# Moving a second context's statistics, some modulation products and the additions of the norms' squares in a fused two-block kernel on one core

## The chip, the core and the metric

The kernel runs on one core of a Trainium2 chip. A core has five engines that run their own instruction streams side by side and meet at semaphores: TensorE (PE in the profile; its weight loads are PEld), VectorE (DVE), ScalarE (ACT), GpSimd (POOL) and SyncE (SP, which here only issues transfers). The metric is the device time of one execution, in microseconds (us); lower is better.

## The reference

Two blocks are computed one after the other on 256 tokens of width 1024, all in float32. A second context `ctx_2` is normalised in the second block only.

```python
def rmsnorm(x, g):
    return x * lax.rsqrt(jnp.mean(x * x, axis=-1, keepdims=True) + EPS) * g

def modulate(h, shift, scale):
    return h * (1 + scale) + shift

# first block, layer 0: x += gate * (even mixer: conv branch and LRU branch, then w_out)
# first block, layer 1: x += gate * (odd mixer):
#     u, g = split(modulate(rmsnorm(x, ..)) @ od_w_in)            tiles "ou" and "og"
#     d    = multiscale_pool(u) - u
#     y    = einsum("bngi,gij->bngj", d, w_grp) * scale * silu(g)  tiles "grp"
#     out  = y @ od_w_out                                          tiles "oa" and "ob"
# x = rmsnorm(x, final_g)

# second block
# mod, mc = silu(c_2) @ w_mod_2 + b, silu(c_ctx_2) @ w_mod_2 + b
# hc = modulate(rmsnorm(ctx_2, g_mix), mc[0], mc[1])
# h  = modulate(rmsnorm(x, g_mix), mod[0], mod[1])
#     both times w_in_2                                           tiles "f", "i", "q", ...
# HGRN2 recurrence, gated unit with a layer norm of v, w_o, residual, rmsnorm
# SwiGLU: tiles "ua", "ub", then w_down; residual, rmsnorm(g_final)
```

## The kernel before, in words

Activations stand feature by feature: `x` is [128 partitions, 8 chunks, 256 tokens], so a chunk is a 128x256 float32 tile and a sum over the model width is a sum over partitions and over the 8 chunks (`KT` is 8). All weights come through one stream of 512 KB tiles, [128, 8, 128], in the fixed list `ORDER`. SP loads them into a ring of six buffers `raw`. For most tiles ACT rounds a copy `w_hi` (L868), DVE makes the rest `w_lo = raw - w_hi` (L1225), and PE makes three matmuls for each of the 8 chunks: high by high (L510), low by high (L511), high by low (L512), 24 for a tile. `thirds("oa", t, ...)` is that for tile t of the weights called "oa"; four banks `ps0` to `ps3` take turns as its results, and four more, `px`, take statistics and small products. The "grp" tiles are used as they come, from `raw` (L645). PE, ACT and DVE each go through their code in a fixed, hand-written order and wait on counting semaphores.

DVE makes `w_lo` a few tiles ahead: `lows(name, t)` makes all that are still missing up to that tile, and `ahead` calls it for the tile four further on, each time DVE is about to wait for a finished tile.

Between the parts of the model that multiply by weights there are norms. For a norm ACT squares the 8 chunks into a buffer (`sq1`, `sq2`, `sqc`, ...), counting `sq_ready`; PE sums them by 8 matmuls with a matrix of ones (`stats`, L474; a float32 matmul of 256 columns is listed as two records); DVE scales the sum (`rstd`, L1542), ACT takes the root (`sqrt_of`, L1056, behind a small activation on `warm`, L1052, that brings in its table), DVE inverts it (L1544), and `modulate` (DVE L1245 and L1250, ACT between them) makes the high and low halves of the next input. The norm of x behind the first block and the one that opens the second block are made together from `sq2` and `sqc` (L1652 to L1660).

The modulation vectors are products of a vector with `mod_w`, 80 tiles of 512 KB in 20 groups of four. POOL issues their loads in the order of `MOD_ORDER` into four buffers `modw` (L434), each when DVE has released that buffer, and DVE multiplies a tile by `c_row` and accumulates (`mod_tiles`, L1259; the second block's with two vectors, `second_mods`, L1580).

In program order, around the change: tiles "yb" with `add_to_x` (L1533) and the squares `sq1`; "ou" (16 tiles); "og" (16 tiles, DVE running `second_mods` beside them); "grp" (8 tiles, 128 matmuls); `stats` of `sqc`, here the squares of the second context `ctx2T`, which ACT makes behind its "grp" loop; "oa" 0 to 3, "ob" 0 to 3, "oa" 4 to 7, "ob" 4 to 7, with `add_to_x`, `sq2` and `sqc` (now squares of x) for each "ob" tile; the first "f" tile on the context; `stats` of `sq2` and of `sqc`; three more "f" tiles on the context and then those tiles on x; the rest of "f" on both. Much later come the sums of `v2` and `vsq` for the layer norm of v (L778, four matmuls each), `sq4` before "ua", and `sq5` at the end.

```python
def stats(bank, squares, ready, signal=sq_ready, tiles=KT, step=1):
    for k in range(tiles):
        pe.wait_ge(signal, ready + step * k + 1)
        last = pe.matmul(bank[:, 0:T], ones, squares(k), start=(k == 0), stop=(k == tiles - 1))
    last.then_inc(stat_done, 1)
```

## Time and profile before

| | before |
|---|---|
| median of 3 runs | 1001.12 us (1000.72 to 1001.75) |
| the profiled execution: time, span | 1004.44 us, 1002.7 us |
| mean granted TensorE clock | 0.957 of full |
| PE busy | 92% of the span |
| DVE busy | 71% |
| ACT busy | 50% |
| POOL busy | 11% |
| DMA, mean | 195 GB/s |

The profile is of one execution. "Busy" counts an engine's own instructions; PE at 92% may still wait at single places, and those are found in the timeline, where a row carries in brackets the idle time ahead of it and what ended it. PEclk is the TensorE clock that was granted, 1.00 for full speed.

### The profile page before, as it was taken

Reading aid. Unit: us, or ns where it says so; the run is one execution under the profiler, and the core shown is the slowest. Engines: PE = TensorE matmul, PEld = TensorE weight load, DVE = VectorE, ACT = ScalarE, POOL = GpSimd, SP = SyncE. Lnnn points to the kernel's source line nnn. Section 1 sums busy time; section 2 is a strip of 40 time slices with the busy share of each in tenths; the row PEclk is TensorE's granted clock in tenths of the full one; section 3 lists DMA queues with packets and bytes.
Section 4 is the critical chain, followed back from the end, with each engine's and each line's share of the span. In section 5 each row is a group of like instructions: output and inputs, shape, how many; then the busy total and the mean of one; then the engine's idle time right before and its main releaser. Section 6 shows DMA issues by size and latency. Waiting matters only on the chain.

```text
span 1002.7 us, 17148 instructions
## 1 busy us (share of the span) xinstructions
PE 920.5 (92%) x7040; PEld 855.5 (85%) x7040; DVE 709.1 (71%) x1061; ACT 501.2 (50%) x723; POOL 105.6 (11%) x212
## 2 busy tenths in 40 slices
PE   6799998798799999898899799998999899999996
PEld 3488676578798999887899799998999799999996
DVE  2986678936946599986755997666797695656543
ACT  4633889674734654224354348374543544444441
POOL 0003866500000000110100210000000000000000
PEclk9699999998799899998999899999999899999998
DMA  9734997942356368883861775453555376666661
GB/s 375 309 110 142 343 295 229 326 137 76 111 184 204 127 181 281 291 280 102 309 183 31 283 254 148 124 193 92 185 187 170 104 254 186 183 179 187 194 204 44
DMA packets 56014, 195.53 MB, mean 195 GB/s; under 512 B 7936, under 2 KB 9088, under 8 KB 54528
## 3 DMA queue, kind: packets, MB, share of 16 engines
q1 hardware_dynamic: 40320, 147.83, 46.1%
q0 software_dynamic: 15616, 46.61, 13.6%
q8 instruction: 56, 0.92, 0.4%
q14 instruction: 22, 0.18, 0.1%
HBM read 188.70 MB, written 1.05 MB: 189 GB/s over the span
## 4 chain that ended last, share of the span: by engine, by line
PE 63%; DVE 18%; DMA 7%; ACT 5%; issue 4%; POOL 2%; SPq 1%; DVEq 0%; ACTq 0%; POOLq 0%
PE ps L510 18%; PE ps L512 18%; PE ps L511 18%; DVE w_lo L1225 4%; DMA modw<-in_mod_w 3%; DVE modw L1259 2%; DMA m<-in_mod_w 2%; PE px L474 2%; POOL shifts L443 2%; DMA raw<-in_stream 2%; ACT w_hi L868 2%; DVE dump L1580 1%; PE ps L578 1%; PE px L567 1%; PE ps L645 1%
## 5 line engine op out<-in xcount | busy, mean ns | idle before, releaser
L1225 DVE TENSOR_TENSOR w_lo<-raw,w_hi 128x1024 fp32r<-128x1024 f32 x232 | 279.7, 1221 | 151.2 <-ACT w_hi L868 150.3
L510 PE MATMUL ps<-h_hi,w_hi 128*128 128x256 f32 (+1 forms) x928 | 281.2, 303 | 41.7 <-DVE w_lo L1225 26.3
L868 ACT ACTIVATE w_hi<-raw 128x1024 fp32r<-128x1024 f32 x232 | 243.3, 1055 | 129.6 <-DMA raw<-in_stream 129.4
L511 PE MATMUL ps<-h_lo,w_hi 128*128 128x256 f32 (+1 forms) x928 | 277.0, 298 | 0.0
L512 PE MATMUL ps<-h_hi,w_lo 128*128 128x256 f32 (+1 forms) x928 | 276.6, 298 | 0.0
L510 PEld LDWEIGHTS ps<-h_hi,w_hi 128*128 128x128 f32 x928 | 185.3, 200 | 52.9 <-DVE w_lo L1225 33.9
L511 PEld LDWEIGHTS ps<-h_lo,w_hi 128*128 128x128 f32 x928 | 185.4, 200 | 3.5 <-issue 0.7
L512 PEld LDWEIGHTS ps<-h_hi,w_lo 128*128 128x128 f32 x928 | 185.2, 200 | 2.7
L510 PE MATMUL ps<-h2o_hi,w_hi 128*128 128x256 f32 x352 | 103.2, 293 | 8.2 <-DVE w_lo L1225 8.2
L434 POOL DMA_DIRECT2D modw<-in_mod_w x80 | 42.8, 536 | 626.1 <-DVE modw L1259 357.8
L512 PE MATMUL ps<-h2o_hi,w_lo 128*128 128x256 f32 x352 | 100.9, 287 | 0.0
L511 PE MATMUL ps<-h2o_lo,w_hi 128*128 128x256 f32 x352 | 100.9, 287 | 0.0
L1259 DVE SCALAR_TENSOR_TENSOR modw<-modw,c_row 128x1024 f32<-128x1024 f32 x64 | 75.5, 1219 | 11.7 <-DMA modw<-in_mod_w 11.6
L510 PEld LDWEIGHTS ps<-h2o_hi,w_hi 128*128 128x128 f32 x352 | 68.9, 196 | 9.4 <-DVE w_lo L1225 8.6
L443 POOL DMA_DIRECT2D shifts<-upad x128 | 62.7, 498 | 73.9 <-DVE upad L1378 66.6
L511 PEld LDWEIGHTS ps<-h2o_lo,w_hi 128*128 128x128 f32 x352 | 68.9, 196 | 0.3 <-issue 0.2
L512 PEld LDWEIGHTS ps<-h2o_hi,w_lo 128*128 128x128 f32 x352 | 68.8, 196 | 0.0
L1043 ACT ACTIVATE sq<-x 128x256 f32<-128x256 f32 x32 | 13.4, 417 | 75.7 <-DVE x L1533 73.9
L510 PE MATMUL ps<-ff_hi,w_hi 128*128 128x256 f32 x176 | 49.8, 283 | 0.0
L511 PE MATMUL ps<-ff_lo,w_hi 128*128 128x256 f32 x176 | 49.8, 283 | 0.0
L512 PE MATMUL ps<-ff_hi,w_lo 128*128 128x256 f32 x176 | 49.8, 283 | 0.0
L510 PE MATMUL ps<-y_hi,w_hi 128*128 128x256 f32 x128 | 37.2, 291 | 3.5 <-DVE w_lo L1225 3.5
(308 smaller groups left out, 1717.9 us busy)
## 6 DMA issues: line engine op xcount, KB each, us to landing
raw<-in_stream SPq DMA_DIRECT2D x252, 512.0 KB, 3.9
modw<-in_mod_w POOLq DMA_DIRECT2D x80, 512.0 KB, 6.0
m<-in_mod_w SPq DMA_DIRECT2D x8, 1024.0 KB, 16.2
shifts<-upad POOLq DMA_DIRECT2D x128, 35.5 KB, 4.9
c_row<-in_c_rows SPq DMA_DIRECT2D x3, 512.0 KB, 7.7
ctxT<-in_ctxT SPq DMA_DIRECT2D x1, 1024.0 KB, 5.1
x<-in_xT SPq DMA_DIRECT2D x1, 1024.0 KB, 7.1
ctx2T<-in_ctx2T SPq DMA_DIRECT2D x1, 1024.0 KB, 7.5
```

Source lines behind the costliest of these rows:

```text
L434: pool.dma_start(modw[j][:], ins["mod_w"][t]).then_inc(modw_in[j], 16)
L443: pool.dma_start(shifts[t % 2][32 * d:32 * d + 32, g, :], upad[32 * g:32 * g + 32, t % 3, d:d + RW]).then_inc(shifts_in[t % 2], 16)
L474: last = pe.matmul(bank[:, 0:T], ones, squares(k), start=(k == 0), stop=(k == tiles - 1))
L510: pe.matmul(o, wh, hi, start=start, stop=False)
L511: pe.matmul(o, wh, lo, start=False, stop=False)
L512: return pe.matmul(o, wl, hi, start=False, stop=stop)
L567: mm = pe.matmul(px[b][:, :], w[:, 4 * e + b, :], xpad[:, head, :, SCONV_LEFT:SCONV_LEFT + T], start=True, stop=True)
L578: mm = pe.matmul(o[c, 0:T], w[:, n, c], shifts[t % 2][:, g, 4 * n:4 * n + T], start=(n == 0), stop=(n == QUADS - 1))
L868: act.activation(w_hi[split[0] % HI_RING][:], raw[n % RING][:], ACT.Copy).then_inc(w_hi_ready, 1)
L1043: act.activation(dst[:, t, :], x[:, t, :], ACT.Square).then_inc(sq_ready, 1)
L1225: v.tensor_tensor(w_lo[n % RING][:], raw[n % RING][:], w_hi[split[0] % HI_RING][:].bitcast(F32), ALU.subtract).then_inc(w_lo_ready, 1)
L1259: v.scalar_tensor_tensor(out=modw[s][:], in0=modw[s][:], scalar=1.0, in1=c_row[:, row, :], op0=ALU.mult, op1=ALU.mult, accum_out=mod[:, t: ...
```

## The change

It has three parts.

1. **Additions on GpSimd.** A new helper `add_up` makes POOL add chunks 1 to 6 of a buffer of squares into chunk 0, one 128x256 addition each, waiting for `sq_ready` of the chunk and for its own addition before. PE then sums two chunks by `two_chunks`: chunk 0 when `added` says that all six additions are made, and chunk 7. So it is for `sq1`, `sqx` (below), `sq2`, `sqc`, `sq4` and `sq5`; `v2` and `vsq` (four chunks) are added up entirely by POOL, three additions each, and PE takes one matmul for each. In all 36 + 6 = 42 additions. They stand in POOL's queue between the `modw` loads of groups 7 and 8 (`sq1`), 10 and 11 (`sqx`), 12 and 13 (`sq2` and `sqc`, taking turns), 16 and 17 (v), 18 and 19 (`sq4`) and behind the last loads (`sq5`).
2. **The context's statistics.** Its squares go to a buffer of their own, `sqx`, and ACT makes them before the tile "og" 10; PE sums them behind the last "og" tile, ahead of "grp"; ACT takes the root and DVE the inverse ahead of their "grp" loops. DVE's `modulate` of the context stands behind its "grp" loop as before, but behind two pieces of `lows` that now stand ahead of it.
3. **The modulation products.** `MOD_ORDER` becomes the plain order: groups 6 and 7 are loaded and multiplied at the "yb" tiles, no longer behind the context's `modulate`. Group 13 is multiplied one tile at a time in the first loop over `Kk`, no longer as one block of four ahead of it.

```diff
-MOD_ORDER = [0, 1, 2, 3, 4, 5, 8, 9, 10, 11, 6, 7] + list(range(12, MOD_TILES // MOD_SLOTS))
+MOD_ORDER = list(range(MOD_TILES // MOD_SLOTS))
...
+            def add_up(bufs, signal, ready, n, step=1):
+
+                before = [0] * len(bufs)
+                for k in range(1, n):
+                    for e, (dst, src) in enumerate(bufs):
+                        pool.wait_ge(signal, ready + (step * k + e + 1 if step else 1))
+                        if k > 1:
+                            M.sync(before[e])
+                        a = pool.tensor_tensor(dst, src[:, 0, :] if k == 1 else dst, src[:, k, :], ALU.add)
+                        if k == n - 1:
+                            a.then_inc(added, 1)
+                        else:
+                            before[e] = M.do(a)
...
+            def two_chunks(bank, squares, n, ready):
+
+                pe.wait_ge(added, n)
+                pe.matmul(bank[:, 0:T], ones, squares[:, 0, :], start=True, stop=False)
+                pe.wait_ge(sq_ready, ready)
+                pe.matmul(bank[:, 0:T], ones, squares[:, KT - 1, :], start=False, stop=True).then_inc(stat_done, 1)
...
                 thirds("og", t, *h1)
+            two_chunks(px[1], sqx, 2, 4 * KT)
...
                 mm.then_inc(tile_done, 1)
-            stats(px[1], lambda k: sqc[:, k, :], 3 * KT)
...
                 if t == 0:
-                    stats(px[0], lambda k: sq2[:, k, :], 4 * KT, step=2)
-                    stats(px[2], lambda k: sqc[:, k, :], 4 * KT + 1, step=2)
+                    two_chunks(px[0], sq2, 4, 6 * KT)
+                    two_chunks(px[2], sqc, 4, 6 * KT)
...
             for t in range(2 * KT):
+                if t == 10:
+                    act.wait_ge(in_ctx2, 16)
+                    act.wait_ge(d_ready, 4)
+                    for k in range(KT):
+                        act.activation(sqx[:, k, :], ctx2T[:, k, :], ACT.Square).then_inc(sq_ready, 1)
                 done("og", t)
...
+            sqrt_of(5, vr[:, 0, :])
             for t in range(KT):
                 done("grp", t)
...
-            act.wait_ge(in_ctx2, 16)
-            for k in range(KT):
-                act.activation(sqc[:, k, :], ctx2T[:, k, :], ACT.Square).then_inc(sq_ready, 1)
-            sqrt_of(5, vr[:, 0, :])
-            highs("oa", 3)
+            highs("ob", 1)
             shifted(KT, h2c_hi, t2, sh2[1])
...
             lows("yb", 1)
+            mod_tiles(6, 1)
...
                 add_to_x("yb", t, gate0)
+                if t < 4:
+                    mod_tiles(7, 1, t, 1)
...
+            rstd(6, px[1][:, 0:T], D, EPS, vr[:, 0, :], vr[:, 3, :], 5)
             for t in range(KT + 1):
...
-            mods_used(10)
+            lows("oa", 3)
+            lows("ob", 1)
+            mods_used(12)
...
-            rstd(6, px[1][:, 0:T], D, EPS, vr[:, 0, :], vr[:, 3, :], 5)
+            S.do(tt_(gate1, mod[:, 3 * KT:4 * KT], col("mod_b", 5 * KT, KT), ALU.add))
             modulate(KT, ctx2T, vr[:, 3, :], sc2[1], sh2[1], t2, h2c_hi, h2c_lo)
-            mod_tiles(6, 1)
-            ahead("oa", 2)
-            mod_tiles(7, 1)
-            mods_used(12)
-            S.do(tt_(gate1, mod[:, 3 * KT:4 * KT], col("mod_b", 5 * KT, KT), ALU.add))
...
-            mod_tiles(13, 0)
...
                     if d:
                         mod_tiles(14 + hd // 2, 0, 2 * (hd % 2), 2)
+                    else:
+                        mod_tiles(13, 0, hd, 1)
```

The added lines push the others down; in the listings below, of the changed kernel, L549 is the old L512, L683 the old L645, L511 and L513 are the two matmuls of `two_chunks`, L458 is the addition, L436 the load, L1262 makes `w_lo`, L1282 and L1287 are the two halves of `modulate`.

On PE, from the last "og" tile to the first "oa" tile, before (the "grp" tiles in between, `ps<-d_in`, are cut to the first and the last):

```order
L512 MATMUL ps<-h_hi,w_lo_58 128x256
L645 MATMUL ps<-d_in,raw_53 128x256 [waits d_ready,ps_free0,raw_in4]
L645 MATMUL ps<-d_in,raw_53 128x256 x7
...
L645 MATMUL ps<-d_in,raw_54 128x256 x7
L474 MATMUL px<-sqc,ones_p 128x256 [waits sq_ready] x8
L510 MATMUL ps<-y_hi,w_hi_65 128x256 [waits y_ready,ps_free0,w_lo_ready]
L511 MATMUL ps<-y_lo,w_hi_65 128x256
```

The same place on PE in the changed kernel:

```order
L549 MATMUL ps<-h_hi,w_lo_58 128x256
L511 MATMUL px<-sqx,ones_p 128x256 [waits added]
L513 MATMUL px<-sqx,ones_p 128x256 [waits sq_ready]
L683 MATMUL ps<-d_in,raw_53 128x256 [waits d_ready,ps_free0,raw_in4]
...
L683 MATMUL ps<-d_in,raw_54 128x256 x7
L547 MATMUL ps<-y_hi,w_hi_65 128x256 [waits y_ready,ps_free0,w_lo_ready]
```

The eight matmuls between "grp" and "oa" are gone, and two stand between "og" and "grp".

On DVE, behind the "grp" loop, before (`px` to `vr` is `rstd`, `t` and `h2c_lo` are `modulate` of the context, `modw,mod` the products of groups 6 and 7, `w_lo_59` to `w_lo_56` the low halves for "ob" 0 to 3):

```order
L1542 TENSOR_SCALAR vr<-px 128x256 [waits stat_done,dve_step]
L1544 RECIPROCAL vr<-vr 128x256 [waits sd_ready]
L1245 SCALAR_TENSOR_TENSOR t_130<-ctx2T,small,vr 128x256 [waits dve_step]
...
L1250 SCALAR_TENSOR_TENSOR h2c_lo<-t_130,small,h2c_hi 128x256 [waits act_hi] x3
L1259 SCALAR_TENSOR_TENSOR modw_67,mod<-modw_67,c_row 128x1024 [waits modw_in0]
...
L1225 TENSOR_TENSOR w_lo_59<-raw_53,w_hi_63 128x1024 [waits w_hi_ready]
L1225 TENSOR_TENSOR w_lo_60<-raw_54,w_hi_64 128x1024 [waits w_hi_ready]
L1225 TENSOR_TENSOR w_lo_55<-raw_49,w_hi_65 128x1024 [waits w_hi_ready]
L1259 SCALAR_TENSOR_TENSOR modw_67,mod<-modw_67,c_row 128x1024 [waits modw_in0]
...
L1225 TENSOR_TENSOR w_lo_56<-raw_50,w_hi_66 128x1024 [waits w_hi_ready,dve_step]
```

And in the changed kernel:

```order
L1668 TENSOR_TENSOR y_lo<-yt,y_hi 128x512 [waits y_rounded,ps_free3]
L1262 TENSOR_TENSOR w_lo_59<-raw_53,w_hi_63 128x1024 [waits w_hi_ready]
L1262 TENSOR_TENSOR w_lo_60<-raw_54,w_hi_64 128x1024 [waits w_hi_ready]
...
L1282 SCALAR_TENSOR_TENSOR t_131<-ctx2T,small,vr 128x256 x3
...
L1287 SCALAR_TENSOR_TENSOR h2c_lo<-t_131,small,h2c_hi 128x256 [waits act_hi] x3
L1262 TENSOR_TENSOR w_lo_55<-raw_49,w_hi_65 128x1024 [waits w_hi_ready,dve_step]
L1262 TENSOR_TENSOR w_lo_56<-raw_50,w_hi_66 128x1024 [waits w_hi_ready]
```

The `rstd` has left this place (it stands ahead of the "grp" loop), the eight products of groups 6 and 7 have left it too, and the low halves of "ob" 0 and 1 stand ahead of `modulate`.

On POOL, the additions for `sqx` between the loads of groups 10 and 11 in the changed kernel; before, the loads follow each other directly:

```order
L436 DMA modw_70<-in_mod_w 128x1024 [waits modw_used3]
L458 TENSOR_TENSOR sqx<-sqx 128x256 [waits sq_ready]
L458 TENSOR_TENSOR sqx<-sqx 128x256 [waits pool_step,sq_ready] x5
L436 DMA modw_67<-in_mod_w 128x1024 [waits modw_used0]
```

The four loads of group 11 now stand behind six additions, which themselves stand behind the fourth load of group 10.

## Rows read from the trace of the kernel before

**Rows 1.** The page, busy time of each engine over the span.
```profile
PE 920.5 (92%) x7040; PEld 855.5 (85%) x7040; DVE 709.1 (71%) x1061; ACT 501.2 (50%) x723; POOL 105.6 (11%) x212
```

**Rows 2.** Waits of PE: who waited for whom, total, times, longest.
```profile
PE ps L510 <- DVE w_lo L1225: 37.9, 19, 6.5
```

**Rows 3.** PE's timeline: start, duration, line, shapes, count; idle before, releaser.
```profile
455.77 1.67 PE L645 MATMUL ps<-d_in,raw 128*128 128x256 f32 x7
461.48 0.79 PE L474 MATMUL px<-sqc,ones_p 128*128 128x256 f32 x1 [4.04 <-ACT sqc L1079]
...
482.83 0.38 PE L510 MATMUL ps<-y_hi,w_hi 128*128 128x256 f32 x1 [3.50 <-DVE w_lo L1225]
...
518.98 0.28 PE L510 MATMUL ps<-h2c_hi,w_hi 128*128 128x256 f32 x1
...
521.86 3.62 PE L474 MATMUL px<-sq,ones_p 128*128 128x256 f32 x16
525.32 3.62 PE L474 MATMUL px<-sqc,ones_p 128*128 128x256 f32 x16
528.58 0.47 PE L510 MATMUL ps<-h2c_hi,w_hi 128*128 128x256 f32 x1
...
567.07 0.58 PE L510 MATMUL ps<-h2o_hi,w_hi 128*128 128x256 f32 x1 [6.46 <-DVE w_lo L1225]
```

**Rows 4.** Windows: length; PE, PEld, DVE, ACT, POOL busy; PEclk, DMA share, GB/s.
```profile
387.00:429.50 42.50, 38.05 (x299) 36.03 (x298) 41.24 (x60) 14.39 (x23) 5.91 (x12) 1.00 0.84 289
461.50:467.50 6.00, 6.00 (x17) 4.84 (x17) 1.24 (x8) 3.55 (x9) 0.00 (x0) 0.55 0.01 3
484.00:486.00 2.00, 2.00 (x12) 2.00 (x11) 2.00 (x2) 0.00 (x0) 0.00 (x0) 0.50 0.97 373
490.00:518.00 28.00, 28.00 (x235) 28.00 (x235) 16.48 (x21) 14.50 (x22) 0.53 (x1) 1.00 0.76 249
...
280.00:284.00 4.00, 4.00 (x36) 4.00 (x35) 0.14 (x1) 0.00 (x0) 0.00 (x0) 1.00 0.00 0
286.00:294.00 8.00, 8.00 (x69) 8.00 (x68) 4.07 (x4) 3.27 (x4) 0.00 (x0) 1.00 0.91 361
```

**Rows 5.** DVE's timeline at the four places that the prediction speaks of.
```profile
470.64 1.27 DVE L1245 SCALAR_TENSOR_TENSOR t<-ctx2T,small,vr 128x256 f32<-128x256 f32 x3
...
475.79 1.27 DVE L1250 SCALAR_TENSOR_TENSOR h2c_lo<-t,small,h2c_hi 128x256 fp32r<-128x256 f32 x3
...
522.26 0.48 DVE L1533 SCALAR_TENSOR_TENSOR x<-ps,small,x 128x256 f32<-128x256 f32 x1
...
560.30 1.22 DVE L1259 SCALAR_TENSOR_TENSOR modw<-modw,c_row 128x1024 f32<-128x1024 f32 x1
...
993.67 0.42 DVE L1542 TENSOR_SCALAR v<-px 128x256 f32<-128x256 f32 x1 [2.97 <-PE px L474]
```

**Rows 6.** ACT's timeline: squares, table warm-up and roots.
```profile
523.15 0.49 ACT L1086 ACTIVATE sqc<-x,cols 128x256 f32<-128x256 f32 x1
...
791.71 0.42 ACT L1056 ACTIVATE v<-v 128x256 f32<-128x256 f32 x1
...
992.51 0.20 ACT L1052 ACTIVATE small<-small 128x1 f32<-128x1 f32 x1
994.12 0.42 ACT L1056 ACTIVATE v<-v 128x256 f32<-128x256 f32 x1 [1.41 <-DVE v L1542]
```

**Rows 7.** PE's timeline at the layer norm of v.
```profile
659.97 1.89 PE L778 MATMUL px<-v,ones_p 128*128 128x256 f32 x8
...
674.80 0.39 PE L510 MATMUL ps<-h2o_hi,w_hi 128*128 128x256 f32 x1 [1.71 <-DVE w_lo L1225]
```

**Rows 8.** DVE groups by line: shapes, count; busy, mean ns; idle before.
```profile
L1225 DVE TENSOR_TENSOR w_lo<-raw,w_hi 128x1024 fp32r<-128x1024 f32 x232 | 279.7, 1221 | 151.2 <-ACT w_hi L868 150.3
...
L1929 DVE TENSOR_TENSOR ff<-ps,sa 128x256 f32<-128x256 f32 x22 | 9.2, 417 | 0.0
```

**Rows 9.** POOL's timeline, the last load of group 10.
```profile
414.93 0.53 POOL L434 DMA_DIRECT2D modw<-in_mod_w  x1 [3.09 <-DVE modw L1580]
```

More of the change, by code:

```diff
@@ L247, in build @@
         sqc = at("sqc", W + 16, [KT, T])
+        sqx = at("sqx", W + 68, [KT, T])
         sq2 = at("sq2", W + 24, [KT, T])
@@ L324, in build @@
         crow_ready = sem("crow_ready")
+        pool_step, added = sem("pool_step"), sem("added")
         sq_ready = sem("sq_ready")
@@ L444, in shifted_copies @@
                                        upad[32 * g:32 * g + 32, t % 3, d:d + RW]).then_inc(shifts_in[t % 2], 16)
+            M = Steps(pool, pool_step)
+            def add_up(bufs, signal, ready, n, step=1):
[10 more added lines that the diff above has]
+                            before[e] = M.do(a)
             copies_after = {0: (0,), 1: (1,), 2: (2, 3), 3: (4, 5), 4: (6,), 5: (7,)}
             for g in range(MOD_TILES // MOD_SLOTS):
+                if g == 17:
+                    pool.wait_ge(sg_act, 1)
+                    add_up([(vn[:, 0, :], v2), (vsq[:, 0, :], vsq)], sg_act, 0, HEADS, 0)
+                elif g == 19:
+                    add_up([(sq4[:, 0, :], sq4)], sq_ready, 6 * KT, KT - 1)
                 for s in range(MOD_SLOTS):
@@ L451, in _ @@
                     shifted_copies(t)
+                if g == 7:
+                    add_up([(sq1[:, 0, :], sq1)], sq_ready, 2 * KT, KT - 1)
+                elif g == 10:
+                    add_up([(sqx[:, 0, :], sqx)], sq_ready, 3 * KT, KT - 1)
+                elif g == 12:
+                    add_up([(sq2[:, 0, :], sq2), (sqc[:, 0, :], sqc)], sq_ready, 4 * KT, KT - 1, 2)
+            add_up([(sq5[:, 0, :], sq5)], sq_ready, 7 * KT, KT - 1)
         @block.tensor
@@ L629, in _ @@
                 thirds("yb", t, *yb, first=False)
-            stats(px[0], lambda k: sq1[:, k, :], 2 * KT)
+            two_chunks(px[0], sq1, 1, 3 * KT)
             h1 = (lambda k: h1_hi[:, k, :], lambda k: h1_lo[:, k, :])
@@ L774, in _ @@
             thirds("o", 1, *own2)
-            pe.wait_ge(sg_act, 1)
-            for n, src in ((0, v2), (1, vsq)):
-                for g in range(HEADS):
-                    last = pe.matmul(px[n][:, 0:T], ones, src[:, g, :], start=(g == 0), stop=(g == HEADS - 1))
-                last.then_inc(sg_pe, 1)
+            for n, src in ((0, vn), (1, vsq)):
+                pe.wait_ge(added, 5 + n)
+                pe.matmul(px[n][:, 0:T], ones, src[:, 0, :], start=True, stop=True).then_inc(sg_pe, 1)
             thirds("o", 2, *own2)
@@ L840, in _ @@
                 thirds("wo", t, lambda k: m_hi[:, k, :], lambda k: m_lo[:, k, :])
-            stats(px[0], lambda k: sq4[:, k, :], 6 * KT)
+            two_chunks(px[0], sq4, 7, 7 * KT)
             h3 = (lambda k: h3_hi[:, k, :], lambda k: h3_lo[:, k, :])
@@ L851, in _ @@
                            ready=(ff_ready, n * KT) if t == 0 else None)
-            stats(px[0], lambda k: sq5[:, k, :], 7 * KT)
+            two_chunks(px[0], sq5, 8, 8 * KT)
         @block.scalar
```

## The prediction, made before the changed kernel ran

> **What bounds the kernel now.** I read the page first: PE is busy 920.5 us of 1002.7, no other engine over 71% [rows 1]. So time can come out only where PE does work that is not needed or where it waits or runs slow. The waits of PE say for what: most of all for DVE's `w_lo`, 37.9 us in 19 waits, the longest 6.5 [rows 2]. The timeline of PE then shows the stretch that the change touches [rows 3]. "grp" ends at 455.77 + 1.67 = 457.44. PE is idle for 4.04 until ACT has squared the context. The sums run at 461.48 and, in the window beside it, at a granted clock of 0.55, seventeen records in 6 us [rows 4]. Four "oa" tiles follow, then a wait of 3.50 for the `w_lo` of "ob" 0, and behind it again half the clock (0.50 from 484 to 486), before full speed. The first "f" tile starts at 518.98 and takes 2.88, the two sums 3.46 and 3.26, and the next tile starts at 528.58. At full speed a tile of 24 matmuls is 521.86 - 518.98 = 2.88, and one matmul with the ones 3.46 / 8 = 0.43. Both times PE had stood idle for about 4 us, and both times it came back at the lower of its two clock levels, 1.2 GHz.
>
> **From "grp" to the second "f" tile.** Before: 528.58 - 457.44 = 71.14. After: two matmuls, 2 x 0.43 = 0.87, now ahead of "grp" and on PE's path; sixteen "oa"/"ob" tiles and one "f" tile without a gap, 17 x 2.88 = 48.96; so the "f" tile ends at 507.27 on the old time scale. The squares are later than that. `add_to_x` of "ob" 7 started at 522.26 and its last square ended at 523.15 + 0.49 = 523.64 [rows 5, 6], 4.66 behind the end of "ob" 7. That lag is made by DVE's and ACT's chain per tile, which the change leaves alone, so the squares end at 504.39 + 4.66 = 509.05. PE can take chunk 0 of `sq2` meanwhile and has three matmuls left, 1.30: the next tile starts at 510.35, 52.9 after "grp" where it was 71.1. **Gain 18.2**. It is made of the wait of 4.04, the eight slow matmuls, the wait of 3.50, the half clock behind it (288 matmuls took 36.15 where 34.56 is full speed) and twelve of the sixteen matmuls behind "f" 0, less the 0.87 moved ahead and the new wait of 1.35.
>
> It needs two things of DVE. The `modulate` of the context takes 475.79 + 1.27 - 470.64 = 6.4 [rows 5], and the `w_lo` of "ob" 2 is now behind it. PE wants that one at 458.3 + 6 x 2.88 = 475.6. DVE ends its "grp" work some 4 behind PE, about 461.5 (ACT's squares, right behind its own "grp" work, let PE go at 461.48), then two `w_lo` (1.14 pitch each), small vectors, `modulate` to about 472.5, `w_lo` to about 474: 1.5 to spare. The `rstd` ahead of the "grp" loop (a scaling, a root and an inverse, about 2.7) makes DVE late for the first "grp" results, but PE has four banks and 3.5 for each of these tiles, so it wants the first bank back 14 after it began; nothing.
>
> **The block of group 13.** PE stands 6.46 for the `w_lo` of "f" 6 [rows 3]; on DVE four products of 1.14 pitch from 560.30 stand ahead of it [rows 5]. Now two of them stand behind it: **gain 2.3**. Later `w_lo` don't give it back: PE needs 5.8 for each "f" tile on both inputs, DVE about 3.9 with its two products.
>
> **The end.** The squares end at 991.2; the last sum releases DVE at 993.67 [rows 5] and the root follows at 994.12. With two matmuls the variance is ready about 1.1 after the squares, before the table is in: the warm-up ends at 992.51 + 0.20 [rows 6], so the root starts at about 992.8. **Gain 1.3**. The same sums at "ua" give nothing: there the root at 791.71 had no wait for the variance at all.
>
> **The layer norm of v.** PE's eight matmuls at 659.97 [rows 7] become two, 2.6 less. But PE waits at 674.80 for a `w_lo` (1.71), at the end of a chain of ACT and DVE that starts from other results at 660; the wait grows by what is saved: **0**. The six additions must be done in the 9 us before 659.97. The loads of group 17 stand behind them and are late, but their products come 50 us later.
>
> **The modulation products at "yb".** The DVE work of groups 6 and 7 lies where DVE is about half busy (4.07 of 8). But group 7's four loads, 2 MB, now start at about 281.7 to 285.1. The DMA is empty from 280 to 284 and carries 361 GB/s at a share of 0.91 from 286 [rows 4]. 2 MB at 361 GB/s are 5.8, of which 3.3 fit ahead of 285: the weight tiles come up to 2.5 later. Two or three rounded tiles lie in stock, so I take a third: **loss 0.8** (0 to 2.5).
>
> **The additions.** No row shows GpSimd computing. DVE does a 128x256 tensor_tensor in 0.42 and one of 128x1024 in 1.22 [rows 8]; I bound the addition by these and take 0.7, between them, as GpSimd need not be as fast as DVE on the same shape. The place that matters is `sqx`: the six additions start after the load at 414.93 [rows 9], in "og", where DVE is busy 41.24 of 42.5 and PE waits for its `w_lo` for each tile [rows 4]. What holds DVE up there by a microsecond costs one. Beside nothing it costs 0; if each addition holds DVE for its own length, 6 x 0.7 = 4.2 (at 1.22, 7.3). I take **4.2**, because a copy of two big streams on DVE and one on GpSimd use the same memory and DVE has no idle time to hide a stop. The other sets stand beside a DVE that is half busy (16.48 of 28 at "ob"): **0.5** for all. Group 11's loads, behind the six, are issued up to 8 late; their buffers are wanted a round of four tiles later, 14 us, and landing takes about 6, so they just fit.
>
> The Trainium skill, "SBUF — State Buffer", on its two separate sides, says that an operation of DVE with two SBUF inputs and one of GpSimd that reads SBUF take one shared port pair as an exclusive lock, and the loser stops for the whole instruction. By that page it would be the 4.2 and not the 0; no run here shows it yet. Its "GPSIMD Engine Reference" measures an addition of 2048 float32 at 4497 ns, by which 256 would be an estimated 0.56 plus a fixed part.
>
> **Sum.** 18.2 + 2.3 + 1.3 - 0.8 - 4.2 - 0.5 = 16.3. The profiled execution took 1004.44, 3.3 over the median of 1001.12; so about 988 if profiled, and 984.8 for the median.
>
> **Rivals.**
> - *No interference* (0.22). The additions run beside DVE without a stop: 21.0 off, **980.1**. For it: nothing in the trace of before has POOL and DVE stop each other, POOL having only loads. Against it: only that DVE and POOL have not been seen to compute at once.
> - *Dear additions* (0.12). At 1.22 each, held in full at "og" (7.3), 1 at "ob", and the load collision at 2.5: **990**.
> - *The waits move in* (0.09). DVE is late behind `modulate` (an ACT that rounds late, 1.5 us to spare only) and PE stops at "ob" 2 as before at "ob" 0, with the half clock behind it: 3.5 + 1.6 come back, **990**.
> - *Slower* (0.03). The length of an addition decides, c. `sqx` costs 6c where it holds DVE. For `sq2` and `sqc` twelve additions have about 28 us from "ob" 1 until PE asks; above 2.3 each PE waits 12c - 28. At c = 3 that is 18 + 8 = 26 against the 21 of gains: about **1006**. It decides from c about 2.7. Against it: seven times what DVE needs.
> - *It does not do what it says* (0.02). PE finds `added` late everywhere by what it saves, since POOL's queue has loads ahead of the additions that wait for DVE: no change. Against it: the last load of group 10 is out at 414.93, and PE asks at 429.65.
>
> **Numbers.** The forecast case has 0.52, with a range of its own of 982 to 987.5. A difference under 0.2% (2 us) can't be told from none. Faster is all but the last two rivals, 0.95; within 0.2% 0.02; slower 0.03. The range reaches from below the case without interference, 978.5, to just past the two at 990, 990.5; it leaves out some 0.1.
>
> **What would show it.** In the changed profile: PE goes from "grp" through the fourth "oa" and "ob" without a gap and with the clock at 1.00; four matmuls with the ones behind "f" 0 where sixteen were, and a wait of about 1.4 for ACT's `sqc` ahead of the last; the wait for `w_lo` at "f" 6 is about 4.2; the root at the end directly behind its warm-up; POOL rows of 128x256 of 0.5 to 1.2 us. In "og", from 415 on, the DVE products and `w_lo` beside additions show 1.9 in place of 1.2, or gaps, if the stop is real, and 1.2 without gaps if not. Wrong I would be if the "og" stretch grew by more than 8, if PE waited for `added`, or if a wait of 3 or more for `w_lo` stood at "ob" 2.

## The result, and the profile after

| | before | after |
|---|---|---|
| median of 4 runs | 1000.92 us (998.77 to 1001.75) | 984.82 us (982.05 to 988.23) |
| ratio | | 0.9844, 95% interval 0.9805 to 0.9883 |
| the profiled execution: time, span | 1004.44, 1002.7 | 988.23, 986.4 |
| clock | 0.957 | 0.957 |

Forecast was 984.8, in a range of 978.5 to 990.5. The same kernel run five more times gave a ratio of 0.9822 (0.9798 to 0.9846). The profiled execution of after is the slowest of its four runs.

The page and the waits of PE after the change, to be read beside [rows 1] and [rows 2]:

```profile
PE 899.5 (91%) x6956; PEld 837.5 (85%) x6956; DVE 713.0 (72%) x1061; ACT 501.7 (51%) x723; POOL 142.9 (14%) x254
...
PE ps L547 <- DVE w_lo L1262: 42.0, 20, 6.2
```

PE is busy 21 us less: 84 records of matmul are gone. It does not wait less for `w_lo`, but more: one wait has gone and others have come. PE's timeline shows which (start, duration, line, shapes, count; idle before and what ended it), to be read beside [rows 3] and [rows 7]:

```profile
297.26 0.39 PE L547 MATMUL ps<-yb_hi,w_hi 128*128 128x256 f32 x1 [2.33 <-DVE w_lo L1262]
...
439.27 0.60 PE L511 MATMUL px<-sqx,ones_p 128*128 128x256 f32 x2
439.70 0.59 PE L513 MATMUL px<-sqx,ones_p 128*128 128x256 f32 x2
440.13 0.38 PE L683 MATMUL ps<-d_in,raw 128*128 128x256 f32 x1
...
467.57 0.47 PE L547 MATMUL ps<-y_hi,w_hi 128*128 128x256 f32 x1
...
513.83 0.28 PE L547 MATMUL ps<-h2c_hi,w_hi 128*128 128x256 f32 x1
...
516.71 0.60 PE L511 MATMUL px<-sq,ones_p 128*128 128x256 f32 x2
517.38 0.70 PE L513 MATMUL px<-sq,ones_p 128*128 128x256 f32 x2
517.92 0.59 PE L511 MATMUL px<-sqc,ones_p 128*128 128x256 f32 x2
518.35 0.59 PE L513 MATMUL px<-sqc,ones_p 128*128 128x256 f32 x2
518.60 0.47 PE L547 MATMUL ps<-h2c_hi,w_hi 128*128 128x256 f32 x1
...
554.79 0.58 PE L547 MATMUL ps<-h2o_hi,w_hi 128*128 128x256 f32 x1 [4.18 <-DVE w_lo L1262]
...
661.31 0.58 PE L547 MATMUL ps<-h2o_hi,w_hi 128*128 128x256 f32 x1 [4.32 <-DVE w_lo L1262]
```

From "grp" to the "f" tile no row has a bracket: the idle 4.04 and 3.50 are gone, and the windows show the clock at 1.00 through both stretches, where before had 0.55 and 0.50 [rows 4] (window, then PE, PEld, DVE, ACT and POOL busy, PEclk, DMA share, GB/s):

```profile
440.00:467.00 27.00, 27.00 (x127) 23.77 (x126) 22.53 (x39) 8.39 (x12) 2.12 (x4) 1.00 0.75 254
468.00:513.00 45.00, 45.00 (x378) 45.00 (x377) 31.43 (x52) 25.03 (x38) 7.20 (x10) 1.00 0.58 180
```

New is the wait of 2.33 at "yb". Times there have to be counted from the start of "ya", which is at 273.76 before and at 277.49 here, 3.7 later. PE waits for `w_lo`, DVE for ACT's `w_hi`, and ACT for a weight tile. ACT's rows, the first from before and the second from after:

```profile
287.99 1.06 ACT L868 ACTIVATE w_hi<-raw 128x1024 fp32r<-128x1024 f32 x1 [9.29 <-DMA raw<-in_stream]
294.89 1.06 ACT L903 ACTIVATE w_hi<-raw 128x1024 fp32r<-128x1024 f32 x1 [12.47 <-DMA raw<-in_stream]
```

So the tile is there 14.2 behind the start of "ya" before and 17.4 behind it after, 3.2 later, though SP issues its next loads 10.63 behind it in both. Group 7's four loads leave 8.1 to 11.6 behind it. A window around PE's wait shows the DMA nearly full and a granted clock of 0.72:

```profile
296.00:302.00 6.00, 4.74 (x27) 4.74 (x28) 3.99 (x5) 2.12 (x2) 0.00 (x0) 0.72 0.95 382
```

And in "og", DVE's timeline beside POOL's six additions:

```profile
421.37 1.22 DVE L1262 TENSOR_TENSOR w_lo<-raw,w_hi 128x1024 fp32r<-128x1024 f32 x1
422.51 1.76 DVE L1620 SCALAR_TENSOR_TENSOR dump<-modw,c_row 128x1024 f32<-128x1024 f32 x1
...
424.38 1.57 DVE L1620 SCALAR_TENSOR_TENSOR modw<-modw,c_row 128x1024 f32<-128x1024 f32 x1
...
425.88 1.73 DVE L1262 TENSOR_TENSOR w_lo<-raw,w_hi 128x1024 fp32r<-128x1024 f32 x1
427.53 1.75 DVE L1620 SCALAR_TENSOR_TENSOR dump<-modw,c_row 128x1024 f32<-128x1024 f32 x1
...
430.89 1.74 DVE L1262 TENSOR_TENSOR w_lo<-raw,w_hi 128x1024 fp32r<-128x1024 f32 x1
432.55 1.21 DVE L1620 SCALAR_TENSOR_TENSOR dump<-modw,c_row 128x1024 f32<-128x1024 f32 x1
```

```profile
422.29 9.25 POOL L458 TENSOR_TENSOR sqx<-sqx 128x256 f32<-128x256 f32 x6
```

While the six additions run (9.25 us for six, 0.74 us each where they stand alone), six DVE operations take 1.56 to 1.76; ahead and behind they take 1.22. That is 2.8 us in all.

At the end the root starts 0.29 behind the start of its warm-up, without a wait for the variance, as against 1.41 of waiting [rows 6]:

```profile
977.62 0.20 ACT L1087 ACTIVATE small<-small 128x1 f32<-128x1 f32 x1
977.91 0.42 ACT L1091 ACTIVATE v<-v 128x256 f32<-128x256 f32 x1
```

The readings below go by parts of the program, since the stretch from the start to "ya", which is the same in all these kernels but for which group of products POOL loads last, took anything from 268.4 to 277.5 us in their profiles (one wait of PE for `w_lo` near 200 us was anything from 0.4 to 5.2). So the medians, whose runs lie 3 to 9 us apart, say less than a part does. Each part ends where the first matmul of the next one starts, the last one where PE's last matmul ends; "sums" are those behind "f" 0. Each row is one profile, and a part that holds a wait can differ by over 1 us for a reason that has nothing to do with the edit: how long PE runs at half its clock behind the wait (see the last section). Of before there is one profile only, 3.5 over its median.

| profile | ya, yb, norm | ou, og, `sqx` | grp, context sum | oa, ob | f 0 to 3, sums | f to i | last tiles, sums |
|---|---|---|---|---|---|---|---|
| before | 54.2 | 101.7 | 37.8 | 51.5 | 18.4 | 69.7 | 67.0 |
| after | 58.1 | 104.6 | 27.4 | 46.3 | 13.6 | 66.1 | 65.3 |
| after, again | 56.8 | 104.3 | 27.4 | 46.3 | 13.7 | 67.4 | 65.3 |
| moves only | 57.1 | 105.3 | 27.4 | 46.3 | 18.4 | 66.3 | 67.0 |
| additions only | 53.6 | 100.7 | 36.0 | 51.5 | 14.5 | 68.4 | 65.3 |
| products back (1st) | 53.6 | 113.5 | 28.4 | 57.7 | 13.6 | 66.9 | 65.3 |
| products back (2nd) | 53.6 | 106.2 | 27.4 | 56.6 | 13.8 | 66.4 | 65.3 |
| group 7 late | 54.7 | 107.5 | 27.4 | 46.3 | 13.7 | 66.4 | 65.3 |
| PE sums `sqx` | 56.9 | 105.2 | 27.4 | 46.3 | 13.7 | 66.4 | 65.3 |
| twelve additions | 58.3 | 107.8 | 31.5 | 46.9 | 14.6 | 67.0 | 65.3 |
| fills | 56.7 | 105.3 | 27.4 | 46.3 | 13.6 | 66.4 | 65.3 |
| products in ob | 54.0 | 104.7 | 27.4 | 46.3 | 28.2 | 66.4 | 65.3 |
| the same, pairs | 54.2 | 104.5 | 27.4 | 46.3 | 18.7 | 67.1 | 65.3 |
| group 13 in a block | 58.4 | 104.4 | 27.4 | 46.3 | 13.6 | 69.5 | 65.3 |

### The profile page after: what moved, and what is told of

Its sections match the earlier page's. It is cut to its first block, busy times and chain, and to the rows that moved or that the text cites. A ratio compares the mean times of both kernels' runs of the same rounds, so it can differ in the third digit from the quotient of the medians.

```text
span 986.4 us, 17057 instructions
## 1 busy us (share of the span) xinstructions
PE 899.5 (91%) x6956; PEld 837.5 (85%) x6956; DVE 713.0 (72%) x1061; ACT 501.7 (51%) x723; POOL 142.9 (14%) x254
## 3 DMA queue, kind: packets, MB, share of 16 engines
q0 software_dynamic: 15616, 46.61, 13.7%
## 4 chain that ended last, share of the span: by engine, by line
PE 62%; DVE 17%; DMA 8%; ACT 6%; issue 3%; POOL 3%; SPq 1%; DVEq 0%; ACTq 0%; POOLq 0%
PE ps L547 18%; PE ps L549 18%; PE ps L548 17%; DVE w_lo L1262 5%; DMA modw<-in_mod_w 3%; PE ps L683 3%; DMA raw<-in_stream 3%; DMA m<-in_mod_w 2%; POOL shifts L445 2%; ACT w_hi L903 2%; DVE modw L1296 2%; DVE dump L1620 1%; PE ps L615 1%; PE px L604 1%; DVE li L1276 1%
## 5 line engine op out<-in xcount | busy, mean ns | idle before, releaser
L1262 DVE TENSOR_TENSOR w_lo<-raw,w_hi 128x1024 fp32r<-128x1024 f32 x232 | 281.5, 1228 | 143.3 <-ACT w_hi L903 142.6
L549 PE MATMUL ps<-h_hi,w_lo 128*128 128x256 f32 (+1 forms) x928 | 276.9, 298 | 0.0
L549 PEld LDWEIGHTS ps<-h_hi,w_lo 128*128 128x128 f32 x928 | 185.0, 199 | 2.7
L549 PE MATMUL ps<-h2o_hi,w_lo 128*128 128x256 f32 x352 | 101.2, 287 | 0.0
L436 POOL DMA_DIRECT2D modw<-in_mod_w x80 | 43.0, 539 | 351.4 <-DVE modw L1296 219.5
L1296 DVE SCALAR_TENSOR_TENSOR modw<-modw,c_row 128x1024 f32<-128x1024 f32 x64 | 76.5, 1232 | 14.2 <-DMA modw<-in_mod_w 14.1
L549 PEld LDWEIGHTS ps<-h2o_hi,w_lo 128*128 128x128 f32 x352 | 69.1, 196 | 0.0
L458 POOL TENSOR_TENSOR sq<-sq 128x256 f32<-128x256 f32 x24 | 19.0, 790 | 337.4 <-ACT sq L1078 337.4
L549 PE MATMUL ps<-ff_hi,w_lo 128*128 128x256 f32 x176 | 49.8, 283 | 0.0
```

What stands on the lines that cost most here:

```text
L436: pool.dma_start(modw[j][:], ins["mod_w"][t]).then_inc(modw_in[j], 16)
L458: a = pool.tensor_tensor(dst, src[:, 0, :] if k == 1 else dst, src[:, k, :], ALU.add)
L549: return pe.matmul(o, wl, hi, start=False, stop=stop)
L1262: v.tensor_tensor(w_lo[n % RING][:], raw[n % RING][:], w_hi[split[0] % HI_RING][:].bitcast(F32), ALU.subtract).then_inc(w_lo_ready, 1)
L1296: v.scalar_tensor_tensor(out=modw[s][:], in0=modw[s][:], scalar=1.0, in1=c_row[:, row, :], op0=ALU.mult, op1=ALU.mult, accum_out=mod[:, t: ...
```

## The experiments

**The changed kernel again.** No edit.

> The changed kernel, unchanged, once more. Its four runs lay between 982.05 and 988.23, wider apart than those of before. The profile of its slowest run has one wait of PE for w_lo of 5.21 at 204 us where before has 1.86, in a stretch ahead of everything that the change touches. If that wait is chance, a new profile shows it back near 1.9 and a time of about 983 (median 984.8 within 1.5). If the change causes it, it stands again at about 5.

984.39 us, ratio 0.9822 (0.9798 to 0.9846). In its profile "ya" starts at 271.6, 5.9 earlier than in the first profile of after, and the wait in question is 2.2. The 5.2 was chance.

**The moves alone, the additions alone.** The first is the changed kernel with `stats` in place of every `two_chunks` and no `add_up`:

```diff
-            two_chunks(px[1], sqx, 2, 4 * KT)
+            stats(px[1], lambda k: sqx[:, k, :], 3 * KT)
...
-                    two_chunks(px[0], sq2, 4, 6 * KT)
-                    two_chunks(px[2], sqc, 4, 6 * KT)
+                    stats(px[0], lambda k: sq2[:, k, :], 4 * KT, step=2)
+                    stats(px[2], lambda k: sqc[:, k, :], 4 * KT + 1, step=2)
```

> The changed kernel without any addition on GpSimd: PE sums 8 chunks (4 for v) as before, all moves stay. Main theory, the moves bring most (the idle 4.0, the slow sums, the wait of 3.5 and the half clock behind it) and the additions some 7 (12 matmuls x 0.43 behind f 0 = 5.2, 1.7 at the end, 2.6 - 2.8 = about nothing at og, 0 to 1.5 at v): about 992. Rival, the additions are what brings it: about 997 or more. Rival, the additions bring nothing, as squares and not sums are late: 985.

The second is the kernel before with `add_up` and `two_chunks` for all sets but the context's.

> The kernel before with the additions alone (sq1, sq2, sqc, v, sq4, sq5; the context's sum stays PE's 8 matmuls at its old place), no moves. Main theory: 5.2 behind f 0 less what is lost to the late squares there (up to 1.3), 1.7 at the end, 0 to 1.5 at v: 6 to 8 off, about 994. Rival, parts depend on each other and the additions alone bring under 2: about 999.

The moves alone: 989.43, ratio 0.9865 (0.9836 to 0.9895). The additions alone: 995.92, ratio 0.9935 (0.9913 to 0.9957). Within their intervals they add up: 13.5 and 6.5 thousandths, and both together gave 17.8. The 5.0 us between the median of the moves alone and that of the changed kernel are somewhat less than the 7 that I had put down for the additions. In the parts, the moves bring 10.4 and 5.2 from "grp" to the end of "ob". Behind "f" 0 the additions bring 4.7 to 4.8 together with the moves (18.4 against 13.6 and 13.7), and 3.9 alone (14.5). At the end they shorten PE's part by 1.7, in every kernel that has them, but the span from the first of the last tiles to the end of the kernel only by 1.3 (76.0 before and with the moves alone, 74.7 in all others). In the first kernel both sums stand behind "f" 0 in full:

```profile
512.94 3.62 PE L476 MATMUL px<-sq,ones_p 128*128 128x256 f32 x16
516.39 3.62 PE L476 MATMUL px<-sqc,ones_p 128*128 128x256 f32 x16
```

In the second PE waits there for the last square:

```profile
521.11 0.70 PE L510 MATMUL px<-sq,ones_p 128*128 128x256 f32 x2 [0.96 <-ACT sqc L1118]
```

**The products of groups 6 and 7 back behind `modulate`.** `MOD_ORDER` and their place as before, `lows` as in the changed kernel:

```diff
             modulate(KT, ctx2T, vr[:, 3, :], sc2[1], sh2[1], t2, h2c_hi, h2c_lo)
+            mod_tiles(6, 1)
+            ahead("oa", 2)
+            mod_tiles(7, 1)
```

> The changed kernel with the products of groups 6 and 7, and their loads, back behind the context's modulate. At yb the profile of after shows PE 4.1 later than before: a wait of 2.3 for w_lo and half the clock behind it. If group 7's loads cause that, it goes (-4.1), and the wait at ob comes back with its slow matmuls and the lag of the squares (+3.5 + 1.6 + 1.2): about 987. If the 4.1 is chance and not the loads, 991.

999.78, ratio 0.9978 (0.9960 to 0.9997): far off the 987 and the 991 that I had written. One reason is my own slip. With the other order the additions of `sqx` stood one group of loads too late in POOL's queue, and PE waited for them:

```profile
437.98 1.22 PE L511 MATMUL px<-sqx,ones_p 128*128 128x256 f32 x2 [9.38 <-POOL sqx L458]
```

So the same again with the additions one group earlier.

> The earlier kernel with groups 6 and 7 back behind modulate, with POOL's additions of sqx one group of loads earlier, so that they start at about 414 to 420 as in the changed kernel. There PE waited 9.4 for them at the start of grp; that wait should be gone. The rest of that run should stay: no wait at yb (ya to ou 53.6), and from the first oa to the f tile 57.7 instead of 46.3, as DVE makes eight products and waits for group 7's loads while PE now comes earlier. About 990, so moving the products is worth some 5 to 8 net of the 3 that it costs at yb. Rival: the 57.7 came from the late additions; then 46 to 52 and 980 to 985.

992.67, ratio 0.9908 (0.9877 to 0.9940), 8.3 over the changed kernel's median of 984.39: the main theory, not the rival. The wait for `added` is gone, "yb" has none either (53.6), and "oa, ob" takes 56.6 instead of 46.3, more than the 51.5 of before. DVE's timeline there, behind the first four products:

```profile
478.17 1.22 DVE L1262 TENSOR_TENSOR w_lo<-raw,w_hi 128x1024 fp32r<-128x1024 f32 x1
480.70 1.23 DVE L1296 SCALAR_TENSOR_TENSOR modw<-modw,c_row 128x1024 f32<-128x1024 f32 x1 [1.31 <-DMA modw<-in_mod_w]
...
484.48 1.23 DVE L1296 SCALAR_TENSOR_TENSOR modw<-modw,c_row 128x1024 f32<-128x1024 f32 x1 [1.30 <-DMA modw<-in_mod_w]
...
487.31 2.36 DVE L1262 TENSOR_TENSOR w_lo<-raw,w_hi 128x1024 fp32r<-128x1024 f32 x2
```

and PE's:

```profile
479.44 0.38 PE L547 MATMUL ps<-y_hi,w_hi 128*128 128x256 f32 x1 [1.98 <-DVE w_lo L1262]
...
488.59 0.58 PE L547 MATMUL ps<-y_hi,w_hi 128*128 128x256 f32 x1 [6.01 <-DVE w_lo L1262]
```

Once PE is no longer held up by the context's sum, the eight products and group 7's loads stand fully in its way: 10.3 us, against some 3 to 4 that the move costs at "yb" (56.8 and 58.1 where the kernels without it have 53.6 to 54.2).

**Group 7 later.** Group 6's products go between the first four `add_to_x` of "yb", group 7's to the first four "ou" tiles, with POOL's additions of `sq1` ahead of group 7's loads.

```diff
-            mod_tiles(6, 1)
...
                 if t < 4:
-                    mod_tiles(7, 1, t, 1)
+                    mod_tiles(6, 1, t, 1)
...
                     emptied(v, "ou", t)
+                    if g == 0:
+                        mod_tiles(7, 1, t, 1)
```

> The changed kernel with the products of group 6 between the first four add_to_x of yb and those of group 7 at the first four ou tiles; POOL makes the additions of sq1 before group 7's loads, so those leave at about 320 instead of 282 to 289. Theory: group 7's loads beside the weight tiles cost the 2.2 to 2.6 wait at yb 2 and the slow matmuls behind it, 3 to 4 in all; it goes and nothing comes back: 3 to 4 under the changed kernel, about 981, from yb's first tile to ou's first about 53.6 and not 56.8 to 58.1. Rival: DVE's own work there and not the loads makes the wait: it stays. Rival: the loads now collide with the ou tiles and the gain goes again: 984.

984.47, ratio 0.9807 (0.9780 to 0.9833). The wait at "yb" is gone (54.7 for the part instead of 56.8 to 58.1), and the next part is 3 longer (107.5), with a new wait at "ou":

```profile
351.30 0.39 PE L547 MATMUL ps<-h_hi,w_hi 128*128 128x256 f32 x1 [1.65 <-DVE w_lo L1262]
```

The first theory was right on the cause at "yb". The kernel also takes the block of group 6's products away from there, so the shorter part alone would not tell the loads from DVE's work. ACT's rows do: its weight tile is there 14.4 behind the start of "ya", as before the change (14.2) and not as in the changed kernel (17.4), with group 7's loads leaving at 46.6 behind it. The third theory, that the loads collide elsewhere, was right on the sum.

**The additions of `sqx`: none, twelve, or fills.** Three kernels: PE sums the 8 chunks; six more additions into a scratch buffer ahead of the six; PE sums, and POOL writes zeros to six scratch chunks.

```diff
+                    for k in (2, 3, 4, 5, 6, 6):
+                        M.do(pool.tensor_tensor(scr[:, k, :], sqx[:, 0, :], sqx[:, k, :], ALU.add))
+                        M.sync()
                     add_up([(sqx[:, 0, :], sqx)], sq_ready, 3 * KT, KT - 1)
```

```diff
-                    add_up([(sqx[:, 0, :], sqx)], sq_ready, 3 * KT, KT - 1)
+                    for k in range(1, 7):
+                        M.do(pool.memset(scr[:, k, :], 0.0))
+                        M.sync()
```

> The changed kernel, but PE sums the 8 chunks of sqx and POOL makes no addition in og. Theory: the six additions stop DVE for 2.8 in all there (0.34 to 0.54 for each of six DVE operations), and PE's six matmuls cost 2.6: no difference, 984, and in og no DVE product over 1.24. Rival, the longer DVE rows in og come from something else: DVE rows of 1.5 to 1.76 stand there again and it is 2.6 slower, 987.

> The changed kernel with six more additions of the same size in og on POOL, into a scratch buffer, ahead of the real six. If GpSimd's additions and DVE's two-input operations shut each other out (Trainium skill, SBUF - State Buffer, two separate sides), twelve DVE operations are each about 0.5 longer, og grows by another 2.8, and the additions end after PE asks, at some 9 us later: the wait for added comes on top. Without a stop, og does not grow and twelve additions of 0.74 take 9, in time. About 987 to 992 by the first, 984 by the second.

> As the kernel in which PE sums the 8 chunks of sqx, but POOL fills six 128x256 scratch chunks with zeros where the additions stood. If only a GpSimd operation that reads SBUF stops DVE (Trainium skill, SBUF - State Buffer), DVE's rows in og keep 1.22 and the time is that of the kernel without the fills, 984. If any GpSimd operation does, the six next to the fills are 0.3 to 0.5 longer and it is 1 to 3 slower.

With PE's sum: 985.92, ratio 0.9818 (0.9793 to 0.9844), no difference, as expected; no DVE row over 1.24 stands in "og", and PE's sum takes its place:

```profile
434.80 3.62 PE L502 MATMUL px<-sqx,ones_p 128*128 128x256 f32 x16
```

The part "ou, og" is 105.2 here and 104.3 to 104.6 with the additions, but that difference arises ahead of them, in the first four "ou" tiles (14.0 against 12.9 and 13.2, at a lower granted clock). From the tile "og" 12, where the additions begin, to "grp" it is 17.5 with the six additions in three profiles and 18.2 in two others (group 7 late; products back, 2nd), 17.3 in all five with PE's sum, and 13.8 in the two with neither.

With twelve: 991.97, ratio 0.9887 (0.9867 to 0.9906), at the upper end of what I had written for additions that stop DVE. Ten DVE operations in a row take 1.56 to 1.75, and from "og" 12 to "grp" it is 20.4, 2.9 more than with six. The wait of PE for `added` that I expected on top did not come. Instead a cost appears that I had weighed at nothing with six: the loads behind the additions leave 106.3 behind the first "ou" matmul, against 95.9 with six, DVE stands 4.66 us in front of a product, and PE's fifth "grp" tile waits for its bank. DVE's timeline, then PE's (the profile names no releaser for either, only "issue"; that the product waits for its load is read from the order of POOL's rows):

```profile
436.31 1.23 DVE L1625 SCALAR_TENSOR_TENSOR modw<-modw,c_row 128x1024 f32<-128x1024 f32 x1 [0.46 <-DVE dump L1625]
...
442.21 1.23 DVE L1625 SCALAR_TENSOR_TENSOR dump<-modw,c_row 128x1024 f32<-128x1024 f32 x1 [4.66 <-issue]
```

```profile
457.34 2.83 PE L688 MATMUL ps<-d_in,raw 128*128 128x256 f32 x12 [3.80 <-issue]
```

With fills: 983.13, ratio 0.9801 (0.9777 to 0.9825). POOL's six fills take 2.18 us, and the DVE rows beside them have their usual length, 1.22 and 1.23. The first:

```profile
417.98 2.18 POOL L481 MEMSET scr<- 128x256 f32 x6
```

```profile
418.22 1.22 DVE L1624 SCALAR_TENSOR_TENSOR dump<-modw,c_row 128x1024 f32<-128x1024 f32 x1
```

So it is additions, which read SBUF, that stop DVE's two-input operations, and not any work of GpSimd, as the Trainium skill has it ("SBUF — State Buffer", its two separate sides). By that page the loser stops for the whole instruction; the rows show DVE stopped for 0.34 to 0.54, less than the 0.74 that an addition takes, and no run here shows for how much of the 0.74 the addition shuts DVE out.

**The products one at a time in the "ob" loop.** From the kernel in which PE sums `sqx`, with `MOD_ORDER` as before the change; the one `gate1` operation is split into one for each "ob" tile:

```diff
             for t in range(KT):
+                mod_tiles(6 + t // 4, 1, t % 4, 1)
+                v.wait_ge(modw_used[t % 4], 11 + t // 4)
+                S.do(tt_(gate1[:, t:t + 1], mod[:, 3 * KT + t:3 * KT + t + 1], col("mod_b", 5 * KT + t, 1), ALU.add))
+                S.sync()
                 add_to_x("ob", t, gate1)
```

> The products of groups 6 and 7 one at a time in the ob loop, each ahead of the add_to_x whose gate it gives, in DVE's idle time of 1.89 per ob tile; MOD_ORDER as before; PE sums the 8 chunks of sqx. Theory: neither the loads at yb (3.2 to 4) nor the block behind modulate (11) costs: yb as in before (53.6), oa to f 46.3 to 48, 3 to 4 under the changed kernel, ratio about 0.979. Rival: the chain of the ob tiles has no room (1.14 and a small sync in 1.89) and the squares end later by up to 8 x 1: the gain is gone.

993.91, ratio 0.9919 (0.9891 to 0.9947), where 3 to 4 under the changed kernel was expected. "ya, yb" and "oa, ob" are as hoped, 54.0 and 46.3, but POOL's twelve additions now stood behind loads that wait for the last products. They ran back to back, and DVE's `w_lo` that began beside them took as long as all of them:

```profile
512.03 9.30 DVE L1260 TENSOR_TENSOR w_lo<-raw,w_hi 128x1024 fp32r<-128x1024 f32 x1 [0.63 <-ACT w_hi L901]
```

```profile
512.05 0.74 POOL L458 TENSOR_TENSOR sq<-sq 128x256 f32<-128x256 f32 x1
512.74 0.72 POOL L458 TENSOR_TENSOR sqc<-sqc 128x256 f32<-128x256 f32 x1
...
519.54 0.71 POOL L458 TENSOR_TENSOR sqc<-sqc 128x256 f32<-128x256 f32 x1
```

```profile
520.30 1.22 PE L509 MATMUL px<-sq,ones_p 128*128 128x256 f32 x2 [10.07 <-POOL sqc L458]
```

The same with the two additions of chunk k right behind the load of "ob" tile k:

```diff
                     loads(g * MOD_SLOTS + s)
+                    k = (g - 11) * MOD_SLOTS + s
+                    if 1 <= k <= 6:
+                        add_pair(k)
```

> The kernel with the products one at a time in the ob loop, with one thing mended: there POOL's twelve additions for sq2 and sqc stood behind group 12's loads, which wait for the last ob products, so they ran back to back at 512 and PE waited 10.1 for them while one w_lo of DVE took 9.3. Now POOL issues the load of ob tile k and then makes the two additions of chunk k. Theory: the wait and the stopped w_lo go (-14 from f's second tile on), yb stays without its wait: 3 under the changed kernel, ratio about 0.979. Rival: pairs of additions stop DVE's now fuller ob loop (2.9 busy of 3.6 per tile), the squares end 1 to 3 later and the ratio is that of the changed kernel, 0.982.

983.48, ratio 0.9828 (0.9789 to 0.9868). The 3 us won at "yb" are given back behind "f" 0 (18.7 instead of 13.7): the "ob" loop on DVE is full, its `w_lo` beside a pair of additions take 1.54 to 1.56, and PE waits twice for squares and sums:

```profile
511.26 0.70 PE L524 MATMUL px<-sq,ones_p 128*128 128x256 f32 x2 [1.79 <-POOL sqc L472]
513.65 1.22 PE L526 MATMUL px<-sq,ones_p 128*128 128x256 f32 x2 [1.69 <-ACT sqc L1136]
```

The rival was right. No version here is shown to beat the changed kernel.

**Group 13 as one block again.**

> The changed kernel with group 13's four products as one block ahead of the Kk loop, as before. Theory: the wait for w_lo at f 6 goes from 4.2 to 6.5 and the clock comes back later: 2.3 to 3.5 slower, 987.5, ratio about 0.985. Rival: the later w_lo are late by what the first is early, no difference.

983.75, ratio 0.9817 (0.9782 to 0.9853): the expected 987.5 did not come, and the median shows no difference at all. The part does show one: 69.5 instead of 66.1 and 67.4, with the wait back at "f" 6:

```profile
548.51 0.58 PE L547 MATMUL ps<-h2o_hi,w_hi 128*128 128x256 f32 x1 [6.87 <-DVE w_lo L1262]
```

## Why the prediction was right

The forecast time was met, and in the main by the mechanism that it gave; its terms were off by up to 3 us, and the errors cancel. That the median fell on the forecast to the tenth is luck. By its own steps:

- *From "grp" to the second "f" tile, 18.2.* PE's parts from "grp" to the x tiles took 107.7 before and 87.3 after; 20.5 less, minus the 0.9 that moved ahead, 19.6. Right, and 1.4 too small. The step that failed is that the squares' lag behind PE, 4.66, stays. After, the last square ended at 517.33 by ACT's timeline, 3.5 behind the end of "ob" 7, and PE did not wait 1.35: its four matmuls and the waits between them took 1.89, where four at full speed are 1.73. The lag goes with the moves: it is 3.5 with the moves alone and 4.4 with the additions alone, and there PE does wait for the last square, 0.96. That DVE in the old "ob" loop was still catching up with groups 6 and 7 is the likely reason; no run isolates it. With the products back the lag is 3.5 and 3.7, but there PE itself stands 6 us and more for a `w_lo` in "ob", in which DVE can catch up.
- *`modulate` would fit ahead of "ob" 2.* It did; no wait stands there.
- *Group 13, 2.3.* The wait fell from 6.46 to 4.18, 2.3 exactly. The part is 2.2 to 3.5 shorter, but how long PE then ran at half its clock differs between profiles of one kernel. Where it ran so for 5.6 to 5.7 us, the part is 69.6 before and 67.4 after, again; where for under 3, it is 68.4 with the additions alone and 66.1 in the first profile of after. Either pair gives 2.2 to 2.3. No median shows this gain by itself.
- *The end, 1.3; "ua", 0.* The last tiles and all behind them took 76.0 before and 74.7 after, 1.3 as foretold. From the first of the "wo" tiles, ahead of the sums at "ua", to the first "ua" tile it is 32.7 before, 33.1 and 32.4 after.
- *The layer norm of v, 0.* PE's wait grew from 1.71 to 4.32 as foretold. The stretch from these sums to the matmuls of the spatial gating is 59.5 with PE's eight matmuls (moves only) and 59.5 with two. It is 61.0 in the profile of before, though the kernel with the moves only has the same waits there; the difference is the clock behind the last of them (last section).
- *Group 7's loads at "yb", a loss of 0.8 (0 to 2.5).* The mis-sized term: 2.6 to 3.9. The loads left when they were expected, 7.9 to 11.6 behind the start of "ya" in the two profiles of after, where 7.9 to 11.3 had been taken. Two steps were too hopeful. The first weight tile came 3.1 to 3.2 late and not up to 2.5. And the tiles in stock hid 0.8 to 0.9 of that and not two thirds: PE waited 2.2 to 2.3. In the first profile PE then also took 7.3 us for two tiles (5.8 at full speed), at half its clock; in the second 5.9, at full clock.
- *The additions.* One takes 0.74 alone (0.7 taken, between the bounds of 0.42 and 1.22). In "og" they cost DVE 2.8 and not 4.2: each DVE operation was stopped for 0.34 to 0.54, less than an addition lasts. With the two matmuls that makes 3.7 from "og" 12 to "grp" (17.5 against 13.8), where PE's own sum makes 3.5. That set of additions brings nothing.
- *The rivals.* No interference is refuted by the rows in "og" and by the twelve additions. The waits moving in did not happen. What is nearest to happening is the one that I had at 0.02, PE waiting for `added`: it stood 9.4 and 10.1 us in two of my own kernels, each time after a move of one group of loads in POOL's queue.

The price that I gave for putting groups 6 and 7 back, 3.5 + 1.6 + 1.2, was too low too: it is 10.3, where "oa, ob" of before was 5.2 over that of after. My reading is that in before part of it was hidden under PE's other waits.

Not settled: what makes the first part of the program vary by 9 us from one execution to the next.

## What to carry to other kernels

A sum over chunks that PE makes ahead of a norm can be taken over by an idle engine chunk by chunk, since only the last chunk is late; it pays where PE's sum was on the path (3.9 to 4.8 and 1.3 here); in "og" it brought nothing, since the additions held up DVE for as long as they spared PE. Work that is moved out of one wait should be priced with the loads that its buffers release and with whatever else was hiding behind that wait, and the place of every addition in a queue of loads has to be counted again when their order changes. Where two engines shut each other out, spread the short operations of the one; twelve back to back stopped the other for their whole length.

## What the runs showed of the hardware that I had not expected

- Twelve 128x256 additions of GpSimd in two alternating chains left no gap, and one DVE `w_lo` of 1.22 us beside them took 9.30 us. In one chain, where each addition waits for the one before, DVE and GpSimd took turns: DVE's operations took 1.56 to 1.76, the additions about 1.54 instead of 0.74. That the gap between two dependent additions is what lets DVE in is an inference from these two cases.
- GpSimd fills of the same size (2.18 us for six) did not lengthen the two DVE operations beside them (1.22 and 1.23).
- The same wait is followed by a lower clock in one execution and not in another. After a wait of 2.15 for `St` in the layer norm's stretch PE ran at 0.50 for 3 us before the change and at 1.00 with the moves alone (the first two windows), and that is 1.5 us of difference. After the wait at "yb" it ran at 0.50 for 3 us in the first profile of after (a wait of 2.33) and at 1.00 in the second (2.22). After the wait of 3.80 with twelve additions it ran at 1.00, after the wait of 4.32 in the first profile of after at 0.50 (the third window). No run here shows what decides it, so two parts with a wait in them are to be compared only with the clock behind the wait beside them.

```profile
685.50:688.50 3.00, 2.96 (x14) 2.96 (x15) 1.12 (x1) 1.55 (x3) 0.00 (x0) 0.50 0.25 96
673.30:676.30 3.00, 3.00 (x26) 3.00 (x27) 1.26 (x2) 2.03 (x3) 0.00 (x0) 1.00 0.28 109
661.00:666.00 5.00, 4.69 (x22) 4.69 (x23) 4.97 (x5) 4.82 (x8) 0.00 (x0) 0.50 0.01 4
```
